# One-hots by VectorE four tokens at once, and the gates of a dense expert layer built between the last 40 of its first products

## The reference, cut to what matters

```python
def peer_ffn(h, wq, sub_keys, eu, ev):
    ...
        st, it = lax.top_k(s, PEER_TOPK)
        ...
        e = jnp.take_along_axis(cidx, pos, axis=-1)      # 8 heads x 16 experts per token
        g = jax.nn.softmax(best, axis=-1)
        u = jnp.take(eu, e, axis=0)
        act = jax.nn.gelu(jnp.einsum("thkd,td->thk", u, t).astype(jnp.float32), approximate=False)
        return jnp.einsum("thk,thkd->td", (g * act).astype(ev.dtype), jnp.take(ev, e, axis=0))
```

## Time and profile before

| | |
|---|---|
| median of three runs | 3429.46 us |
| the profiled execution | 3425.08 us |
| its span | 3423.2 us (1.9 us lie around it) |
| the layer's U products, gates, V products | about 1036 to 1616, 1722 to 1903, 1904 to 2347 us |
| mean granted clock of TensorE | 0.933 |

### The profile page before, as it was taken

One profiled execution on the slowest core, in us unless ns is written; L12 is line 12 of the kernel. 1 busy time (PEld: TensorE's weight loads), 2 busy tenths in 40 slices (PEclk: granted clock), 3 DMA queues, 4 the chain that ended last, 5 costly groups with the idle time before them and its releaser, 6 DMA issues. The chain is left out here.

```text
span 3423.2 us, 48390 instructions
## 1 busy us (share of the span) xinstructions
PE 3111.7 (91%) x17340; PEld 2550.8 (75%) x17340; DVE 2355.1 (69%) x4543; ACT 1121.3 (33%) x2140; POOL 1057.5 (31%) x712
## 2 busy tenths in 40 slices
PE   9999999999989999388067999998989999999998
PEld 8788889987778888377056444445878999998887
DVE  7554647668745999755699655555774988975555
ACT  5344424543422111011045100002544444444554
POOL 4556118300000344645643545443004930000000
PEclk9999999999989999789555899998989999999999
DMA  7666855531123899899866899995314544445554
GB/s 272 226 235 233 297 188 194 168 131 65 50 81 135 305 338 330 305 349 386 272 193 181 319 388 389 385 380 206 107 47 149 180 158 148 147 156 194 192 194 139
DMA packets 211819, 754.16 MB, mean 220 GB/s; under 512 B 23456, under 2 KB 29216, under 8 KB 211616
## 3 DMA queue, kind: packets, MB, share of 16 engines
q1 hardware_dynamic: 135184, 480.59, 40.1%
q0 software_dynamic: 73728, 268.47, 22.1%
q10 hardware_dynamic: 2704, 2.38, 0.2%
HBM read 748.20 MB, written 1.05 MB: 219 GB/s over the span
## 5 line engine op out<-in xcount | busy, mean ns | idle before, releaser
L2292 POOL DMA_INDIRECT ring_hi<-in_u_rows,arena x256 | 293.2, 1145 | 748.7 <-DVE arena L2583 385.2
L275 PE MATMUL bank<-H,ring 128*128 128x256 f32 x2304 | 500.9, 380 | 5.5 <-ACT arena L2434 2.8
L275 PEld LDWEIGHTS bank<-H,ring 128*128 128x128 f32 x2304 | 438.7, 191 | 66.7 <-ACT arena L2434 3.2
L2497 DVE SCALAR_TENSOR_TENSOR H<-ring_hi,arena,H 128x1024 f32<-128x1024 f32 x254 | 326.6, 1286 | 222.7 <-DMA ring_hi<-in_v_rows,arena 219.5
L2354 PE MATMUL bank<-ring,arena 128*128 128x512 f32 x1024 | 442.1, 595 | 1.4 <-DVE arena L2602 1.4
L290 POOL TENSOR_TENSOR ring_r<-ring,ring_hi_r 128x1024 fp32r<-128x1024 f32 x133 | 321.2, 2417 | 362.5 <-ACT ring_hi_r L284 362.4
L2491 DVE CUSTOM_DVE_ANT_1 ring_hi<-ring_hi,H 128x1024 f32<-128x1024 f32 x256 | 318.0, 1246 | 101.8 <-DMA ring_hi<-in_u_rows,arena 100.3
L2354 PEld LDWEIGHTS bank<-ring,arena 128*128 128x128 f32 x1024 | 195.4, 191 | 247.5 <-issue 245.8
L2292 POOL DMA_INDIRECT ring_hi<-in_v_rows,arena x256 | 291.6, 1139 | 274.5 <-DVE H L2497 243.1
L284 ACT ACTIVATE ring_hi_r<-ring 128x1024 fp32r<-128x1024 f32 x235 | 247.4, 1056 | 299.1 <-PE bank L302 247.0
L2908 ACT ACTIVATE ring_hi_r<-ring 128x1024 fp32r<-128x1024 f32 x260 | 275.4, 1059 | 167.4 <-PE bank L2846 167.2
(11 more groups left out here) (505 smaller groups left out, 6480.9 us busy)
## 6 DMA issues: line engine op xcount, KB each, us to landing
ring<-in_peer_u SPq DMA_DIRECT2D x256, 512.0 KB
ring<-in_peer_v SPq DMA_DIRECT2D x256, 512.0 KB
ring<-in_w_in SPq DMA_DIRECT2D x135, 512.0 KB
arena<-in_ada SPq DMA_DIRECT2D x96, 512.0 KB, 5.5
ring<-in_w_f SPq DMA_DIRECT2D x72, 512.0 KB
ring<-in_w_br SPq DMA_DIRECT2D x24, 512.0 KB
ring<-in_w_out SPq DMA_DIRECT2D x24, 512.0 KB
ring<-in_w_q SPq DMA_DIRECT2D x24, 512.0 KB
```

The lines of the kernel that those rows point to most:

```text
L275: mm = pe.matmul(out_ap, col(n, kt), rhs(kt), start=(kt == 0), stop=(kt == KT - 1))
L2292: pool.indirect_dma_start(G[:, j % NH, :], None, rows, bass.IndirectOffsetOnAxis(ap=idx_u[:, c:c + 1], axis=0)).then_inc(g_in[j % NH], 16)
L2497: ins = dve.scalar_tensor_tensor(tokens(n), rows, act_[:, c:c + 1], tokens(n), ALU.mult, ALU.add)
```

## The change

1. TensorE: `G0 = 88`. The 64 quads are spread over U blocks 88 to 127 (`first_row[q]`, one or two quads per block, 1.6 on average), and `build(q)` is issued just before `up(first_row[q])`. The V blocks wait for `a_rest` and `v_late` in place of `v_g`.
2. A quad built before block f can gate only the rows of S that exist, 0 to f - 1 (`gate`). ScalarE copies the gates of the rows f to 127 from the bank into S (`keep_rest`), and `gelu_late(c)` writes the Gelu of the tokens already built into a buffer `late` (4 x 256), which VectorE's `gate_late(c)` multiplies into S; the other tokens are written into S directly.
3. One-hots: VectorE compares the columns of four tokens at once, straight into `hotB`, then the rows into `hotA`; ScalarE multiplies `hotB` by the shares in place, one Copy with a scale for each token (`weighted_keys`). The first two quads are weighted before `gelu(82)`.
4. Steps: VectorE spends to step 134 (`FIRST`) in place of 250, then one step per quad and one per U block from 88 on (104 steps), then the rest.
5. From gather 242 (`MORE_SLOTS`) on there are seven slots: the four of `G`, and `hotA`, `hotB` and `late`, which are free by then. Gather 242 waits for the last build and the last late gate.

```diff
-                BEFORE = 250
+                G0 = 88
+                first_row = [G0 + q * (NK - G0) // QUADS for q in range(QUADS)]
+                FIRST = PICKS + 6
+                MORE_SLOTS = FIRST + QUADS + NK - G0 + NH
...
+                def slot_of(j):
+                    return j % NH if j < MORE_SLOTS else (4, 5, 6, *((MORE_SLOTS + i) % NH for i in range(NH)))[(j - MORE_SLOTS) % 7]
...
                             if k == 0:
                                 pool.wait_ge(v_idx, n + 1)
-                            if j >= NH:
-                                pool.wait_ge(spent, j - NH + 1)
+                            if j == MORE_SLOTS:
+                                pool.wait_ge(g_ps, QUADS)
+                                pool.wait_ge(v_late, NK - G0)
+                            if sharers(j):
+                                pool.wait_ge(spent, sharers(j)[-1] + 1)
...
                             if q >= 4:
-                                pe.wait_ge(v_g, q - 3)
+                                pe.wait_ge(a_rest, q - 3)
...
                         for c in range(NK):
+                            for q in quads_at(c):
+                                build(q)
                             up(c)
...
-                        pe.wait_ge(a_t, TT)
-                        for q in range(QUADS):
-                            build(q)
-                        pe.wait_ge(v_g, QUADS)
+                        pe.wait_ge(a_rest, QUADS)
+                        pe.wait_ge(v_late, NK - G0)
                         for c in range(NK):
                             down(c)
...
                         def weighted_keys(q):
-                            if q >= 2:
-                                act.wait_ge(g_ps, q - 1)
-                            for u in range(2):
+                            act.wait_ge(v_col, q + 1)
+                            for u in range(4):
                                 t = 4 * q + u
-                                act.activation(hotB[:, q % 2, u, :], cc("iota"), ACT.Abs, bias=cols_[:, t:t + 1],
-                                               scale=-1.0).then_inc(a_far, 1)
-                            for u in range(2):
-                                t = 4 * q + u
-                                act.wait_ge(a_far, 2 * q + u + 1)
-                                w = act.activation(hotB[:, q % 2, u, :], hotB[:, q % 2, u, :], ACT.Relu, bias=wts[:, t:t + 1],
-                                                   scale=neg[:, t:t + 1])
+                                w = act.activation(hotB[:, q % 2, u, :], hotB[:, q % 2, u, :], ACT.Copy, scale=wts[:, t:t + 1])
                             w.then_inc(a_col, 1)
...
+                        def gelu_late(c):
+                            t = 4 * built(c)
+                            act.wait_ge(blocks_done, n0 + u0 + c + 1)
+                            if c >= G0 + 4:
+                                act.wait_ge(v_late, c - G0 - 3)
+                            g = act.activation(late[:, c % 4, 0:t], bank[4 + c % 4][:, 0:t], ACT.Gelu)
+                            if t < T:
+                                g = act.activation(S[:, c, t:], bank[4 + c % 4][:, t:T], ACT.Gelu)
+                            g.then_inc(a_gelu, 1)
+
+                        def keep_rest(q):
+                            act.wait_ge(v_g, q + 1)
+                            f = first_row[q]
+                            act.activation(S[:, f:, 4 * q:4 * q + 4],
+                                           bank[q % 4][:, :].rearrange("p (t k) -> p k t", t=4)[:, f:, :],
+                                           ACT.Copy).then_inc(a_rest, 1)
...
-                        for c in range(FREE, NK):
+                        weighted_keys(0)
+                        weighted_keys(1)
+                        for c in range(FREE, G0):
                             gelu(c)
-                        for q in range(QUADS):
-                            weighted_keys(q)
+                        for c in range(G0, NK):
+                            for q in quads_at(c):
+                                keep_rest(q)
+                                if q + 2 < QUADS:
+                                    weighted_keys(q + 2)
+                            gelu_late(c)
...
-                        while step[0] < BEFORE:
-                            spend()
                         dve.wait_ge(a_t, TT)
                         hit_rows(0)
                         hit_rows(1)
-                        dve.wait_ge(a_gelu, NK)
-                        for q in range(QUADS):
-                            gate(q)
-                            if q + 2 < QUADS:
-                                hit_rows(q + 2)
+                        while step[0] < FIRST:
                             spend()
+                        for c in range(G0, NK):
+                            for q in quads_at(c):
+                                gate(q)
+                                if q + 2 < QUADS:
+                                    hit_rows(q + 2)
+                                spend()
+                            if c > G0:
+                                gate_late(c - 1)
+                            spend()
+                        gate_late(NK - 1)
                         while step[0] < STEPS:
                             spend()
```

More of the change, by code:

```diff
@@ L2235, in build @@
                 act_ = A.take(PEER_H * TOPK)
-                neg = A.take(T)
+                late = A.take(4, T)
                 flat = S.rearrange("p c t -> p (c t)")
@@ L2260, in build, with quads_at, built, sharers @@
                 STEPS = TT * 2 * PICKS
-                BEFORE = 250
+                G0 = 88
+                first_row = [G0 + q * (NK - G0) // QUADS for q in range(QUADS)]
+                def quads_at(c):
+                    return [q for q in range(QUADS) if first_row[q] == c]
+                def built(c):
+                    return sum(f <= c for f in first_row)
                 n0 = used[0]
                 u0, v0 = 16, 16 + NK
+                FIRST = PICKS + 6
+                MORE_SLOTS = FIRST + QUADS + NK - G0 + NH
+                slots = [G[:, i, :] for i in range(NH)]
+                slots += [hotA.rearrange("p a b c -> p (a b c)"), hotB.rearrange("p a b c -> p (a b c)"),
+                          late.rearrange("p a t -> p (a t)")]
                 def tokens(n):
                     return H[:, 4 * n:4 * n + 4, 0, :]
+                def slot_of(j):
+                    return j % NH if j < MORE_SLOTS else (4, 5, 6, *((MORE_SLOTS + i) % NH for i in range(NH)))[(j - MORE_SLOTS) % 7]
+                def sharers(j):
+                    return [x for x in range(j) if slot_of(x) == slot_of(j)]
+                def landed(j):
+                    return 16 * (len(sharers(j)) + 1)
                 with Phase("keys_in", "by_q", "n_normed", "n_high", "xt_ps", "a_xt", "s_ps", "a_s", "v_read", "v_diff", "a_e",
-                           "a_far", "v_idx", "v_found", "t_ps", "a_t", "v_chain", "a_gelu", "a_col", "v_hot",
-                           "g_ps", "v_g", "spent", "a_act", "g_in0", "g_in1", "g_in2", "g_in3") as (
+                           "v_col", "a_rest", "v_late", "v_idx", "v_found", "t_ps", "a_t", "v_chain", "a_gelu", "a_col", "v_hot",
+                           "g_ps", "v_g", "spent", "a_act", "g_in0", "g_in1", "g_in2", "g_in3", "g_in4", "g_in5", "g_in6") as (
                         block, keys_in, by_q, n_normed, n_high, xt_ps, a_xt, s_ps, a_s, v_read, v_diff, a_e,
-                        a_far, v_idx, v_found, t_ps, a_t, v_chain, a_gelu, a_col, v_hot,
+                        v_col, a_rest, v_late, v_idx, v_found, t_ps, a_t, v_chain, a_gelu, a_col, v_hot,
                         g_ps, v_g, spent, a_act, *g_in):
@@ L2289, in gather @@
                                 pool.wait_ge(v_idx, n + 1)
-                            if j >= NH:
-                                pool.wait_ge(spent, j - NH + 1)
+                            if j == MORE_SLOTS:
[3 more added lines that the diff above has]
+                                pool.wait_ge(spent, sharers(j)[-1] + 1)
                             pool.indirect_dma_start(
-                                G[:, j % NH, :], None, rows,
-                                bass.IndirectOffsetOnAxis(ap=idx_u[:, c:c + 1], axis=0)).then_inc(g_in[j % NH], 16)
+                                slots[slot_of(j)], None, rows,
+                                bass.IndirectOffsetOnAxis(ap=idx_u[:, c:c + 1], axis=0)).then_inc(g_in[slot_of(j)], 16)
                         for j in range(STEPS):
@@ L2487, in spend @@
                                 pick_weights(n)
-                            rows = G[:, j % NH, :].rearrange("p (a t) -> p a t", a=4)
-                            dve.wait_ge(g_in[j % NH], 16 * (j // NH + 1))
+                            rows = slots[slot_of(j)].rearrange("p (a t) -> p a t", a=4)
+                            dve.wait_ge(g_in[slot_of(j)], landed(j))
```

(14 more changed lines are left out.)

1 line of the change is left out of this document (removed).

## The result

The changed kernel took 3316.56 us (median of four runs, 3312.24 to 3321.05) against 3427.59 for the kernel before (3414.82 to 3431.39): a ratio of 0.9683, with a 95% interval from 0.9651 to 0.9714. I had forecast 3366, with 3335 as the lower end. It is faster, as forecast, but by 111 us in place of 59. The profiled execution took 3321.05 us (before 3425.08), its span is 3319.2.

A forecast was written before the change was run, and what follows sets the result against it. VectorE was taken to bound the gates, late gathers the phase's end: V products start 170 us earlier, 111 go to waiting for gathers, 59 us less, 3425.1 to 3366; 8 in 10 for 3335 to 3410.

The forecast's parts named there:

- Part 3: V products and after: 442 us with 195 steps beside, 79 steps left alone at 1.5 us, end 2295, 59 us less.
- the sentence on the step count: V stage before: 2.27 us a step beside V blocks, 383 GB/s, taken as full DMA engines, not the four slots.
- The last sentences of the prediction: V stage: if its 2.27 us a step came from slots, the tail would be shorter, the time below the range.
- my 1.5 us each: Rows gathered alone after the V products: price per step, the middle of GpSimd's 1.41 to 1.56 us.
- Part 1: Start of the new stage: eight weighting Copies at 0.4 us delay it 3.2 us; first gate at about 1482.
- Part 2: Gates among U products: VectorE bounds at 248 us plus 5 of waits; V products start at 1735, 170 us earlier.
- Rival D, the clock,: Gates stage: TensorE at half clock throughout, stage 391 us, time 3504; chance 0.08 in full, 0.06 in part.
- Rivals A and B: A: gates stage waits more, 280 us, 3393. B: seven slots bring nothing in the tail, 1.91 us, 3399. Together 0.28.
- Rival C: V stage and tail: DMA stays full to the end at 386 GB/s, end 2273, time 3344; chance 0.12.
- Rival E: Whole phase: all of TensorE's 170 us earlier start arrives, time 3255; chance 0.02.

The follow-up runs named there:

- four_slots: The changed kernel with four gather slots to the end in place of seven, all else left; 3397.66 us, ratio 0.9937 to the kernel before.
- three_tokens_scalar: The changed kernel with ScalarE making the weighted columns of three tokens and VectorE those of one; 3302.69 us, ratio 0.9646, and 3303.5 us again.
- fewer_steps: The changed kernel with one gathered row per quad in the stage of the gates and none per U block; 3319.75 us, ratio 0.9707.

## Why the prediction was wrong

**The step that failed** is in Part 3: "More slots cannot help there, since the DMA engines are full". With it stood the sentence on the step count, that the 383 to 386 GB/s "is a full DMA system, not the four slots". The rate was that of four open gathers, and `four_slots` against the changed kernel shows it: 195 and 224 steps, 382 and 417 GB/s, with the same order and the same V products. I read the busy share of 1.00 as a limit. It is 1.00 at 382 and 1.02 at 417 GB/s, and in the tail of the changed kernel, where VectorE sets the pace, it is 0.99 at 381. The earlier trace rows already had 398 GB/s at 1.01. The last sentences of the prediction had named this case, but I gave it no rival and no chance.

The trace of the kernel before had the sign. GpSimd's waits for a slot to be spent, 1904 to 2346 us (total, times, longest):

```profile
POOL ring_hi L2292 <- DVE H L2497: 136.3, 99, 3.3
...
POOL ring_hi L2292 <- DVE arena L2491: 73.9, 54, 2.9
```

153 of the 197 gathers of that stage waited for VectorE to free a slot, 210 us in all, while VectorE waited for rows. That is what a ring with too few slots does. It doesn't prove it by itself: with seven slots GpSimd still waits 78 us for slots. But it was reason enough to give the slots a rival.

Its price, in the profiled executions: 29 steps more beside the V products, at my 1.5 us each, are 44 us. V products began at 1739.3 in place of 1735, 4 us later; the tail ran at (2253.2 - 2181.6) / 50 = 1.43 us in place of 1.5, 3 us. 2295 + 4 - 44 - 3 = 2252, where the trace has 2253.2. The 1.5 was the middle of GpSimd's bounds; from 2194 us on GpSimd issued a gather each 1.39 us (1.08 busy, 0.30 between), no slower than VectorE spent them. The remaining 3 us of the 104 in the profiled time lie behind the phase, and the profiled run is 4.5 us above its median.

**Part 1** was right in kind: the restart came 5.84 us after the transposes (1467.46 to 1473.30), before 3.67, so 2.2 us later and not 3.2; a Copy with a scale took 0.3, not 0.4. The first gate started at 1483.8, forecast 1482.

**Part 2** held. Groups by line from 1483 to 1739.3 us, the counterpart of the earlier trace rows:

```profile
L2543 DVE SCALAR_TENSOR_TENSOR H<-ring_hi,arena,H 128x1024 f32<-128x1024 f32 x104 | 133.4, 1282 | 12.3 <-DMA ring_hi<-in_v_rows,arena 11.6 <-issue 0.3
...
L2377 PE MATMUL bank<-arena 128*128 128x128 f32 x512 | 72.3, 287 | 38.3 <-DVE arena L2639 36.1 <-issue 1.6 <-ACT arena L2452 0.2
L2639 DVE TENSOR_TENSOR arena<-CS,arena 128x512 f32<-128x512 f32 x62 | 42.7, 688 | 0.0
L2637 DVE TENSOR_TENSOR arena<-CS,arena 128x512 f32<-128x512 f32 x62 | 42.6, 687 | 0.0
...
L2654 DVE TENSOR_TENSOR arena<-arena 128x8 f32<-128x8 f32 (+39 forms) x40 | 11.7, 292 | 0.0
```

The column compare (L2637) costs what the row compare does (L2639), `gate_late` 0.29 us. TensorE waits for VectorE, 36.1 us in all, not the other way round. Waits for rows were 11.6 us, within my 0 to 30. The stage took 256 us, forecast 253. That VectorE bounds it is shown by `three_tokens_scalar` and `fewer_steps`, which take 22 and 50 us of work from VectorE and shorten it by 15 and 56 us (the second has no waits for rows either; TensorE is busy there for 197 of 201 us, so it is the next bound).

**Rival D, the clock,** came in part, as it was priced for one block. A timeline of TensorE (weight loads left out):

```profile
1596.91 1.32 PE L2377 MATMUL bank<-arena 128*128 128x128 f32 x8 [2.16 <-DVE arena L2639]
...
1598.02 5.16 PE L275 MATMUL bank<-H,ring 128*128 128x256 f32 x16
...
1603.91 3.62 PE L275 MATMUL bank<-H,ring 128*128 128x256 f32 x16
```

After a gap of 2.16 us a U block takes 5.16 in place of 3.62 us; the next is at full speed. The mean clock of the stage is 0.95. VectorE paid 2.1 us of waiting for the gate matmuls in the whole stage, all of it at the first gate, so the slack did take it up. In `fewer_steps`, where TensorE has hardly a gap, the clock of the V stage that follows is 1.00 from its start, and its first V products are not slower.

The swinging clock that the Trainium skill describes for another kernel (TensorE: Matmul & The Clock Gate, section A second HAM failure mode: psum-queue depth-cycling) is thus there, and of the 138 us that it could have cost by my estimate, the trace shows next to none, since another engine was the bound. The old stage of the gates, which I had called in agreement, was no case of it: its clock didn't swing but stayed at half (0.51).

**Rivals A and B** didn't occur: 256 us for the stage, and 1.43 us in the tail; B's 1.91 is what `four_slots` shows (1.93). **Rival C** was below my range's middle and still too high: its 386 GB/s was the same mistake. Redone with the 417 GB/s of the runs, 207.6 MB are 498 us, and from 1739 the end would be 2237; the tail's 1.43 us a step, VectorE's own pace of 1.39 and a little, leaves it at 2253. **Rival E** fell, as `fewer_steps` shows.

**What stays open.** With four gathers open, four steps take 4 x 2.27 = 9.1 us; with five open, five take 10.1, with six 11.8, with seven 13.8. From six to seven that grows by one step's 1.97 us, which is what a full resource does. Most of it lies between issue and landing. The median of that time for the U rows that went into the three added slots, with four, five and six open (seven slots each):

```profile
arena<-in_u_rows,arena POOLq DMA_INDIRECT x56, 7.4
```

```profile
arena<-in_u_rows,arena POOLq DMA_INDIRECT x56, 8.0
```

```profile
arena<-in_u_rows,arena POOLq DMA_INDIRECT x56, 9.6
```

So it was not a fixed latency up to a limit, as my theory for five had it. The rest of the round, some 2 us, holds VectorE's step of 1.2 us; the remainder was not divided further. Why the busy share is 1.00 with 35 GB/s to spare is shown only in part. The two queues of `four_slots` (1735 to 2177 us) and of the changed kernel (1738 to 2181):

```profile
q0 software_dynamic: 28204, 102.73, 60.8%
q1 hardware_dynamic: 18168, 66.15, 38.8%
```

```profile
q0 software_dynamic: 32385, 117.95, 65.5%
q1 hardware_dynamic: 18247, 66.42, 36.8%
```

The share is the time that packets took. By these rows a packet took 0.608 x 16 x 442 / 28204 us = 152 ns in the first and 143 in the second, in the other queue 151 and 143: with fewer gathers open the same packets took longer, and so the engines looked as busy at the lower rate. What made them take longer isn't shown.

## What to carry to other kernels

When a stream that runs through several open transfers is late, look whether the issuing engine waits for slots while the consumer waits for data, and try one more buffer before calling the transfer engines full: their busy share of 1.00 left 9% of the throughput unused here, and one or two more buffers took it. Count the steps of each bound separately, and ask how many are left when the other one ends: a start 59 us earlier, bought with 40 steps, was worth nothing; three slots more were worth 4 us in the one order and some 80 in the other (3397.66 against 3316.56). If two edits lift two bounds that end within 7 us of each other, neither shows its worth alone.

## What the runs showed of the hardware

The DMA engines' throughput with two queues of 4 KB packets was flat at 417 to 421 GB/s with six or seven gathers open beside the V blocks, and wavered between 340 and 417 with four. The slices of the V stage of the changed kernel, 1738 to 2181 us:

```profile
GB/s 320 399 419 419 420 420 420 418 419 420 420 420 418 420 420 420 420 418 420 418 421 419 418 420 420 420 419 418 420 420 420 420 417 420 420 420 420 418 420 420
```

That evenness is what a full resource looked like; the wavering in the kernel before, with a mean of 386 in the earlier trace rows, was the sign that I passed over. The V blocks were never late beside seven open gathers: TensorE's 442 us stayed.
